# Output projection of a transformer trunk: tile pairs as seven block products for eight

## The reference, cut to what matters

```python
def merge(p, o_a, o_b, o_c, o_m, w_o):
    parts = [o.reshape(lead + (-1,)) * jax.nn.silu(p[g]) for o, g in ...]
    return jnp.concatenate(parts, axis=-1) @ w_o        # 1024 -> 1024
# x = x + merge(...);  then RMSNorm for the next layer or for y
```

## Time and profile before

| | |
|---|---|
| median of 3 runs | 1696.82 us (1696.16 to 1698.08) |
| the profiled execution | 1696.26 us, span 1694.5 us |
| TensorE busy | 1673.4 us, 99% |
| DVE busy | 1011.9 us, 60% |
| ACT busy | 651.9 us, 38% |
| GpSimd busy | 238.7 us, 14% |
| HBM traffic | 102 GB/s over the span |

### The profile page before, as it was taken

One profiled execution on the slowest core, in us unless ns is written; L12 is line 12 of the kernel. 1 busy time (PEld: TensorE's weight loads), 2 busy tenths in 40 slices (PEclk: granted clock), 3 DMA queues, 4 the chain that ended last, 5 costly groups with the idle time before them and its releaser, 6 DMA issues.

```text
span 1694.5 us, 27274 instructions
## 1 busy us (share of the span) xinstructions
PE 1673.4 (99%) x9431; PEld 1044.2 (62%) x9431; DVE 1011.9 (60%) x2701; ACT 651.9 (38%) x1529; POOL 238.7 (14%) x452
## 2 busy tenths in 40 slices
PE   9999999999999999999999999999999999999998
PEld 4466666766678655555454666667666786555553
DVE  4747888788877233333245288887888762333322
ACT  3632334333343344544134323343333433445531
POOL 2232321100000100002021423220000001000010
PEclk9999999999999999999999999999999999999999
DMA  9343324122222322113422523241232123221130
GB/s 341 151 169 100 128 94 144 42 78 106 90 87 94 118 74 100 33 50 104 145 105 64 170 79 128 91 144 42 78 110 103 71 97 117 72 94 50 38 105 38
DMA packets 46375, 171.25 MB, mean 101 GB/s; under 512 B 11472, under 2 KB 11952, under 8 KB 43040
## 3 DMA queue, kind: packets, MB, share of 16 engines
q1 hardware_dynamic: 29632, 130.68, 22.9%
q0 software_dynamic: 16608, 38.83, 6.9%
HBM read 141.83 MB, written 30.73 MB: 102 GB/s over the span
## 4 chain that ended last, share of the span: by engine, by line
PE 70%; DVE 23%; issue 3%; ACT 1%; DVEq 1%; DMA 1%; ACTq 0%
PE psX L984 48%; DVE lower L1415 16%; PE psT L897 7%; PE psX L1160 5%; PE psS L1093 5%; DVE work L1662 3%; PE psS L1012 2%; DVE gate L1495 1%; PE psX L897 1%; DMA wring<-in_w 1%; ACT gate L1220 0%; DVE gate L1676 0%; PE psS L897 0%; DVE gate L1694 0%; DVE over L1576 0%
## 5 line engine op out<-in xcount | busy, mean ns | idle before, releaser
L984 PE MATMUL psX<-wring,hT 128*128 128x512 f32 (+2 forms) x2016 | 830.2, 557 | 3.8 <-ACT kv L1268 2.1
L984 PEld LDWEIGHTS psX<-wring,hT 128*128 128x128 f32 x2016 | 366.0, 190 | 330.7 <-issue 322.9
L1415 DVE TENSOR_SCALAR_CACHE_REDUCE lower<-sc,thr 128x640 uint8<-128x640 f32 (+5 forms) x462 | 407.3, 933 | 16.8 <-issue 8.6
L984 PE MATMUL psX<-hT,wring 128*128 128x256 f32 (+1 forms) x1600 | 326.1, 359 | 4.3 <-ACT gate L1305 3.8
L1347 ACT ACTIVATE work<-work,stat 128x256 f32<-128x256 f32 (+7 forms) x288 | 200.1, 695 | 303.6 <-DVEq L1665 301.2
L984 PEld LDWEIGHTS psX<-hT,wring 128*128 128x128 f32 x1600 | 274.8, 190 | 37.0 <-issue 7.3
L1356 ACT COPY work<-psT 128x512 f32<-128x512 f32 (+2 forms) x352 | 156.7, 487 | 313.1 <-PE psT L897 312.1
L897 PEld LDWEIGHTS psT<-con,work 128*128 128x128 f32 x1080 | 121.7, 140 | 69.2 <-issue 60.9
L897 PE MATMUL psT<-con,work 128*128 128x128 f32 x1080 | 158.2, 278 | 0.0
L1662 DVE CUSTOM_DVE_ANT_0 work<-psS,bias 128x640 f32<-128x640 f32 (+7 forms) x120 | 86.2, 718 | 44.1 <-issue 22.4
L1710 POOL DMA_DIRECT2D scratch_oscr<-gate x54 | 30.5, 566 | 402.0 <-DVEq L1696 349.5
(11 more groups left out here) (224 smaller groups left out, 1502.7 us busy)
## 6 DMA issues: line engine op xcount, KB each, us to landing
wring<-in_w SPq DMA_DIRECT2D x16, 2048.0 KB, 9.2
cache<-in_kB SPq DMA_DIRECT2D x16, 512.0 KB, 6.5
cache<-in_vB SPq DMA_DIRECT2D x16, 512.0 KB, 4.0
cache<-in_kC SPq DMA_DIRECT2D x16, 512.0 KB, 5.9
cache<-in_vC SPq DMA_DIRECT2D x16, 512.0 KB, 4.6
scratch_oscr<-gate POOLq DMA_DIRECT2D x54, 128.0 KB, 2.0
hT<-scratch_oscr SPq DMA_DIRECT2D x18, 384.0 KB, 3.1
kv<-in_x SPq DMA_DIRECT2D x9, 512.0 KB, 5.5
```

The costliest lines, as they stand in the source:

```text
L984: mm = pe.matmul(out, lhs, rhs, start=(kt == 0), stop=(kt == KT - 1))
L1415: v.tensor_scalar(lower[:, at:at + STRIP_L[t]], sc[:, o], thr[:, n:n + 1], 0.0, ALU.is_lt, ALU.add, accum_out=below[:, n:n + 1])
```

## The change: what it does

For each pair of prompt tiles (2p, 2p+1) and each chunk O0 and O1, the 256 x 1024 by 1024 x 512 product is cut into 2 x 2 blocks (rows: the two tiles; channels: k-tiles 0 to 3 and 4 to 7; columns: two halves of 256). Seven products of 128 x 512 by 512 x 256 take the place of eight, in Strassen's scheme in Winograd's form. Steps "G" are the products, steps "Sh" four sums of rows of `hT` on DVE (for O0 only, and O1 uses them again), steps "Tw" four sums of weight quarters on GpSimd. DVE adds each product into all the quarters of the residual tiles where it belongs.

```diff
+ADDED_TO = [[(0, LEFT)], [(0, WHOLE), (1, WHOLE)], [(1, LEFT)], [(0, RIGHT), (1, WHOLE)], [(0, RIGHT), (1, RIGHT)],
+            [(1, WHOLE)], [(0, RIGHT)]]
...
+                elif k == "G":
+
+                    c, p, n = s[1:]
...
+                    if (p, n) == (0, 2):
+                        pe.wait_ge(*w_combined.on((c, 3)))
+                    if c == "O0" and n >= 3:
+                        pe.wait_ge(*rows_combined.on((p, max(n - 3, 1))))
+                    pe.wait_ge(X.empty(s).sem, X.free(s))
...
+                    lhs, rhs = [(upper[:, LAST_LINES, :], w_quarter(c, LAST_LINES, 0)),
+                                (upper[:, FIRST_LINES, :], w_quarter(c, FIRST_LINES, 0)),
+                                (lower_[:, LAST_LINES, :], t4),
+                                (s2, t2),
+                                (s1, t1),
+                                (s3, t3),
+                                (s4, w_quarter(c, LAST_LINES, 1))][n]
+                    for kt in range(KT // 2):
+                        mm = pe.matmul(X.ap(s)[:, 0:W], lhs[:, kt, :], rhs[:, kt, :],
+                                       start=(kt == 0), stop=(kt == KT // 2 - 1))
```

On DVE (row sums and additions) and GpSimd (weight sums):

```diff
+                    out, a, b, op = [(s1, lower_[:, FIRST_LINES, :], lower_[:, LAST_LINES, :], ALU.add),
+                                     (s2, s1, upper[:, FIRST_LINES, :], ALU.subtract),
+                                     (s3, upper[:, FIRST_LINES, :], lower_[:, FIRST_LINES, :], ALU.subtract),
+                                     (s4, upper[:, LAST_LINES, :], s2, ALU.subtract)][i]
+                    v.tensor_tensor(out, a, b, op)
...
+                    for i, (c0, c1) in ADDED_TO[n]:
...
+                        last = v.tensor_tensor(x, X.ap(s)[:, 0:W].unsqueeze(1).to_broadcast([P, c1 - c0, W]), x, ALU.add)
+                    last.then_inc(X.empty(s).sem, 1)
...
+                    out, a, b = [(t1, b12, b11), (t3, b22, b12), (t2, b22, t1), (t4, b21, t2)][i]
+                    g.tensor_tensor(out, a, b, ALU.subtract).then_inc(w_combined.sem, 1)
```

The sums lie in places that are free by then: O0's weight sums in `qT` and the strips of `sc`, O1's in the sample cache, whose next loads (layer 1's index cache) therefore wait for the last O1 unit:

```diff
+        free = at[(0, ("P", "A1", 2))] if n < RING else at[(loads[n - RING][0], loads[n - RING][1][0])]
+        if l and u[0][0] == "is":
+            free = max(free, at[(l - 1, ("P", "O1", ST_))])
+        put(free, l, "CL", u)
```

The order of the work changes. Units of M1 and A2 take two packs where the queue holds enough, and A's sample packs run with A2's units, so that three packs are left when O0 begins:

```diff
+    def project(c, t, two_packs=False):
+
+        time = pace[0] / (4 if two_packs else 2)
+        select(time)
+        if two_packs:
+            emit("Pp", c, t, 0, 1)
+            operands()
+            emit("Pp", c, t, 1, 3)
+            odd_heads()
+            select(time)
+            emit("Pp", c, t, 3, 4)
+            settle()
+            advance(queue.pop(0) if queue else None)
+            select(time)
+            emit("Pp", c, t, 4, 5)
+            operands()
+            emit("Pp", c, t, 5, 7)
...
+            project(c, t, c in ("M1", "A2") and len(queue) > 1)
...
+        outs = [("O0", 0), ("O0", 1), ("O1", 0), ("O1", 1), ("O0", 2), ("O1", 2), ("O0", 3), ("O0", ST_), ("O1", 3), ("O1", ST_)]
...
+        def multiply(c, p):
+
+            for n in range(7):
+                if c == "O0" and n < 4:
+                    emit("Sh", p, n)
+                emit("G", c, p, n)
+                if n == 1:
+                    operands()
+                if n == 3:
+                    odd_heads()
+                if n in (1, 3) or (n in (4, 6) and c == "O1"):
+                    turn_normed()
+                if n in ((4, 6) if c == "O0" else (1, 3)):
+                    normalize()
...
+                c, p = outs.pop(0)
+                if p == ST_:
+                    turn_normed()
+                    normalize()
+                    normalize()
+                    project(c, p)
+                    turn_normed()
...
+                else:
+                    multiply(c, p)
```

More of the change, by code:

```diff
@@ L154, in program_order @@
     pace = [0.0]
+    queue = []
     def emit(*s, ahead=0):
@@ L174, in turn_units @@
             if t == ST_:
+                assert not any(p[0] == "M" and is_sample(p) for p in queue)
                 emit("Q", ("A", "s0", 0, 1))
@@ L349, in program_order, with normalize @@
                     queue.append((c[0], f"s{j}", j, 1))
-        queue += [("A", f"s{j}", j, 1) for j in range(PAIRS)]
-        outs = [("O0", 0), ("O0", 1), ("O1", 0), ("O1", 1)] + [(c, t) for t in range(2, 7) for c in ("O0", "O1")]
-        outs += [("O0", 7), ("O0", 8), ("O1", 7), ("O1", 8)]
-        to_norm, normed = [], []
[L355 to L359, removed]
+            if (c, t) == ("A2", 6):
+                for i in range(4):
+                    emit("Tw", "O0", i)
+            if c == "A2" and t in A2_ORDER[:PAIRS]:
+                j = A2_ORDER.index(t)
+                queue.append(("A", f"s{j}", j, 1))
+        outs = [("O0", 0), ("O0", 1), ("O1", 0), ("O1", 1), ("O0", 2), ("O1", 2), ("O0", 3), ("O0", ST_), ("O1", 3), ("O1", ST_)]
+        to_norm, normed = [], []
+        def normalize():
             if to_norm:
@@ L366, in program_order, with turn_normed @@
                     normed.append(t)
-            done = [s for s in o if s[0] == l and s[1][0] in ("V", "GT")]
-            ready = lambda t: (l, ("GT", "A")) in done if t == ST_ else (l, ("V", packs_of("A", t)[-1])) in done
-            if outs and ready(outs[0][1]):
-                c, t = outs.pop(0)
-                project(c, t)
+        def turn_normed():
+            if normed:
+                emit("turn", normed.pop(0), ahead=1)
+        def multiply(c, p):
[4 more added lines that the diff above has]
+                if n == 1:
+                    operands()
+                if n == 3:
[4 more added lines that the diff above has]
+                    normalize()
+        for i in range(4):
+            emit("Tw", "O1", i)
+        while queue or pipe != [None, None] or gather or outs or to_norm:
+            work = bool(queue) or pipe != [None, None] or bool(gather)
+            if work:
+                advance(queue.pop(0) if queue else None)
+            done = {s[1] for s in o if s[0] == l and s[1][0] in ("V", "GT")}
+            ready = lambda p: ("GT", "A") in done if p == ST_ else all(
+                ("V", packs_of("A", t)[-1]) in done for t in (2 * p, 2 * p + 1))
+            if outs and ready(outs[0][1]):
+                c, p = outs.pop(0)
[5 more added lines that the diff above has]
+                    turn_normed()
+                    if last and c == "O0":
+                        emit("half", p, ahead=1)
+                else:
+                    multiply(c, p)
                 if c == "O1":
-                    to_norm.append(t)
-                elif last and t == ST_:
-                    emit("half", t, ahead=1)
+                    to_norm += [p] if p == ST_ else [2 * p + 1, 2 * p]
             else:
                 operands()
-            if normed and outs:
-                emit("turn", normed.pop(0), ahead=1)
+                normalize()
             if work:
@@ L436, in tile_uses @@
             out.append((l, ("r", s[2])))
+        elif s[:2] == ("G", "O0") and s[3] == 0:
+            out += [(l, ("r", t)) for t in (2 * s[2], 2 * s[2] + 1)]
     return out
@@ L640, in encoder @@
         norms = events(["norm"], lambda s: s[1])
-        outs = [(l, s[1:]) for l, s in steps("P") if s[1][0] == "O"]
+        outs = []
+        for l, s in steps("P", "G"):
+            if s[0] == "P" and s[1][0] == "O":
+                outs.append((l, s[1:]))
+            elif s[0] == "G" and s[3] >= 5:
+                outs.append((l, (s[1], 2 * s[2] + ADDED_TO[s[3]][0][0])))
         gain_loaded = Signal(sem("gain_loaded"), [(l + 1, "g") for l in range(DEPTH)], lambda e: 16)
@@ L851, in _ @@
                     use, kind, r = u
+                    if l and use[0] == "is":
+                        sums_read = ("P", "O1", ST_)
+                        sp.wait_ge(*X.fill(sums_read, l - 1).on(sums_read, l - 1))
                     done = cache_loaded[cslot[l, u]].sem
```

89 lines of the change are left out of this document (77 added, 12 removed).

## The result

The changed kernel takes **1724.68 us** (median of 4 runs, 1724.45 to 1727.71), the kernel before 1696.49 beside it (1695.16 to 1698.08): a ratio of 1.017, 95% interval 1.0152 to 1.0187, so 28.2 us slower. The profile's page alone doesn't say why.

What follows compares the result with a forecast made beforehand. TensorE, really streaming and busy 99% of 1694.5 us, was taken as the bound. The terms summed to +1.4 on the profiled 1696.3, 1697.7, and with 0.5 added 1698.2 us; own range 1691 to 1706, overall range 1680 to 1711.

Steps and rivals of the forecast that it cites:

- third rival: The change doesn't save: 256-column products run an eighth slower, so seven cost what eight did; 1724 us, chance 0.04.
- Seven for eight: Output units' tile pairs, both layers: seven 256-column products replace eight, 1.64 us saved sixteen times, -26.3 us.
- the second: Rival: each of 112 products pays for its accumulator hand-over, 0.10 us bare each, +11.2 us; 1709 us, chance 0.17.
- The residual: Sample tile's residual load, layer 0, queues behind layer 1's A1 weights, so TensorE waits: +10 us; layer 1 +1.
- clock: TensorE at half speed after idling, taken after the 10 us residual stand: +1.5 us, between 0 and 2.6.
- The first rival: The two queue waits are short: residual lands in 3.9 us, index loads spread; 1683.7 us, chance 0.33.
- Tile 0's turn: Layer 0, O1's second pair: tile 0 is normalised and turned after product 4, chain partly uncovered; +2.2 us, bounds 0 and 4.
- The samples' waits: TensorE's bare waits for the gathered sample tile vanish as sample packs run with A2's units: -3.0 us.
- Layer 1's index caches: Eight 256 KB loads queue late, ahead of the b_f load that DVE's first A1 step needs: +6 us, bounds 1 and 10.
- Two packs per unit: M1 and A2, 11 of 18 units per layer: thinner cover delays V's and unit starts; +6 us, bounds 0 and 12.
- Weight sums: GpSimd's four sums per column half make two or three DVE row sums late by 1 to 2 us: +3 us, bounds 0 and 12.
- additions: DVE adds products into x, covered by TensorE in sum but tight on two accumulators in sixteen places: +1 us.

Runs made afterwards that it cites:

- e4: Changed kernel with tile 4 turned two k-steps into layer 0's O0 unit of the sample tile, so its residual loads before layer 1's A1 weights: 1713.35 us.
- e3: Changed kernel with layer 1's b_f (2 KB) loaded during layer 0's B1 units instead of behind layer 1's eight index caches: 1713.04 us.
- e9: Changed kernel with two packs in ten units (M1 of tiles 6 and 7, all of A2 but tile 4) in place of eleven: 1716.28 us.
- e5: Changed kernel with GpSimd's weight sums of O1 started only after the second pair's last row sum: 1715.93 us.
- e1: Changed kernel's whole order of work, but eight plain products per tile pair, without row sums or weight sums: 1726.84 us.
- e2: Changed kernel with each V in the accumulator bank that the unit around or before it does not hold: 1740.15 us.
- e6: Changed kernel with each GpSimd weight sum of 1024 elements made as four of 256, same places and start: 1718.78 us.

## Why the prediction was wrong

Its sign was nearly a toss-up, and the sum of +1.4 came out as +28.2. That the third rival's number, 1724, is nearly the measured one is chance: its mechanism, slower products, isn't there. By its own steps:

- **Seven for eight, -26.3:** right. The clean pairs run at 0.216 us a matmul. The third rival falls, and so does the second: where DVE is on time, a product has no gap.
- **The residual, +10 and clock +1.5:** right in mechanism and in all but its parts. The load was issued 0.9 us behind the unit's end (838.2) and landed 7.4 later, so 8.3 after the end where I had 12; the stand was 6.7, but the slow clock behind it cost 3.1, over my bound of 2.6. (That bound was misread: eight matmuls at 0.81 in place of 0.43 are 3.0 us, and the row of those matmuls shows a granted clock of 1.00, so it was no good witness for half speed.) Together 9.8; without it (e4) the kernel gained 11.3, some 9 of it here. In layer 1 the term was 0.4, not 1. The first rival falls with it.
- **Tile 0's turn, +2.2:** 2.4 measured, and some 1.7 of clock that the step did not count. **The samples' waits, -3.0:** -3.7.
- **Layer 1's index caches, +6:** right mechanism, size off. The stand was 8.0, b_f landed 10.7 us after its issue, and the clock fell. Without it 11.7 (e3). I had granted slow clock to one stand only. Behind four of layer 0's stands (2.7, 2.4, 6.7 and 8.0 us) the granted clock was 0.5, while it stayed at 1.00 behind M1's stands of 2.40 us and layer 1's two of 1.7. The Trainium skill ("TensorE: Matmul & The Clock Gate", "What's actually happening") says that an idle TensorE falls back to the slower clock; these rows agree for the two long stands, and of the short ones for some only.
- **Two packs per unit, +6:** this step failed. I priced 28 V's at 0.15 us and 2 us for "behind DVE's selection rounds in M1". The V's were no later than said (0.13 at most, but for the one of 1.0 a layer), but the units' first matmuls stood 6.9 us a layer. With the 1.0 that is 15.8 in both, outside my upper end of 12. I had named the accumulator that the V before just used, and not followed it on DVE: V's op is queued behind the gate op of the unit just ended, which waits for ACT's copies, and in M1 behind rounds of 1.2 us. In the stands of 0.7 us and more it ends 2.1 to 3.8 us after the unit's last product (1404.42 to 1408.18 above), and only V, scores and a turn (1.5 us in M1, 2.1 in A2) lie between. e9 shows where this bites: by the stands in its trace about half went when the second packs left the units in which DVE selects. Why the other half stays in A2 was read from the rows; no run removed it.
- **Weight sums, +3, and additions, +1:** failed too. The delay of a row sum was nearly right ("late by 1 to 2 us each": 1.36, 0.56 and 1.43 in layer 1), and it is O1's sums that collide. But I converted it at 3 us for both layers. In the first pairs the stands and their clock were 12.7 us (5.4 and about 7.3), because DVE also had A's logits and the last unit's rotation there: the 128x32 rotation op of 2.35 us above waited for O0's last sum, which I had not put beside it. The additions that hold the accumulators are queued behind all of this. I had compared 7.9 us of DVE work with 12.1 of TensorE's for a pair and not drawn up DVE's queue in the first. e5 gave back 8.8, 7.6 of it in the first pairs; the 2.9 and 2.4 that stay in them are DVE's queue without GpSimd's sums of O1.

So two terms, two packs (+10) and the first pair (weight sums and additions, +9), and the size and clock of the b_f wait (+4 to 6) make most of the difference. In both of the large ones the wait had been seen, and priced by its own length rather than by what is queued behind it.

## What to carry to other kernels

When a change thins the work between two uses of a buffer, write down the releasing engine's queue at that point, in order, with what its head waits for; a sum of busy time over the stretch hides it. Keep GpSimd's operations out of stretches where DVE works on two SBUF operands and TensorE waits for DVE, or cut them small. A load that a change delays should be checked for small loads queued behind it: moving 2 KB ahead of eight loads of 256 KB was worth some 12 us here. And when gains of single experiments are added, look whether the same stretch of slow clock is in several of them.

## What the runs showed of the hardware

A DVE op of 128x32 elements, 0.19 us by itself, took 2.35 us in the shadow of a GpSimd sum; GpSimd's sums took 2.60 to 2.80 us in place of 2.36 beside DVE's row sums, so each waits for the other. The slow clock is not a fixed price of a stand: the same stand of 2.38 us at tile 0's turn was followed by a stretch at 0.5 (1.2 GHz) in the changed kernel, e1, e2, e3 and e6, and by none in e4, e5 and e9, of which e4 runs the same steps up to there. The stand of 2.40 us in M1 was followed by full clock in both layers of the changed kernel. Where DVE sets the pace the slow stretch also costs less than half its length: in e4, which kept full clock there, the first pair of layer 0 stood longer instead (0.96 and 0.40 us at the next products).
